# Computing the second branch gate in the recurrent block and parking it in DRAM

## The reference

```python
u = rms_norm_2(h, norm_mix_g[l])
proj = u @ w_in[l]
x_rnn, g_rnn, q_c, kv_c, k_pe, gate_logits = jnp.split(proj, split_points, axis=-1)
xa = causal_conv(x_rnn, conv_w[l], conv_b[l])
ya = rg_lru(xa, ...) * jax.nn.gelu(g_rnn)
yb = mla(q_c, kv_c, k_pe, positions, ...)
gates = jax.nn.sigmoid(gate_logits.astype(jnp.float32)).reshape(B, S, N_BRANCH, D_MODEL)
merged = gates[:, :, 0] * ya.astype(jnp.float32) + gates[:, :, 1] * yb.astype(jnp.float32)
h = h + merged.astype(h.dtype) @ w_out[l]
```

## Time and profile before

| | us |
|---|---|
| median of 3 runs | 3211.88 |
| lowest and highest | 3197.32, 3213.42 |
| profiled execution | 3216.03 |
| its span | 3214.2 |
| mean granted clock of TensorE | 0.942 |

### The profile page before, as it was taken

The page is one execution under the profiler, slowest core; times in us unless marked ns, Lnnn a source line. Parts: engine busy times, 40 slices in busy tenths (PEclk is TensorE's granted clock), DMA queues, the critical chain, the costliest instruction groups (busy, mean ns, idle before and its releaser), DMA issues. The chain is left out here.

```text
span 3214.2 us, 35213 instructions
## 1 busy us (share of the span) xinstructions
PE 2864.6 (89%) x13216; PEld 2177.6 (68%) x13216; DVE 1801.3 (56%) x2575; ACT 1037.1 (32%) x1329; POOL 211.3 (7%) x186
## 2 busy tenths in 40 slices
PE   4999999999999997949998979899999989479993
PEld 3887778787877884737776955657565568357772
DVE  4677777877632313264444257667575773456663
ACT  3233332333321213244444122212131231246661
POOL 0010111100100000000000010000000000422213
PEclk8999999999999997969999979999999999689996
DMA  4332212232325110121110200000100111779996
GB/s 142 115 108 96 95 66 96 97 109 77 126 97 187 47 33 23 30 92 37 43 46 27 70 14 22 14 22 1 36 1 14 53 35 68 284 250 350 353 362 244
DMA packets 167102, 319.82 MB, mean 100 GB/s; under 512 B 17511, under 2 KB 125160, under 8 KB 153240
## 3 DMA queue, kind: packets, MB, share of 16 engines
q1 hardware_dynamic: 151352, 279.81, 25.3%
q0 software_dynamic: 14720, 34.64, 2.8%
q10 hardware_dynamic: 864, 3.15, 0.2%
HBM read 288.70 MB, written 95.96 MB: 120 GB/s over the span
## 5 line engine op out<-in xcount | busy, mean ns | idle before, releaser
L464 PE MATMUL PS<-UHI,WHI 128*128 128x512 f32 x1008 | 415.4, 412 | 30.0 <-DVE arena L786 15.5
L464 PE MATMUL PS<-ULO,WHI 128*128 128x512 f32 x1008 | 402.6, 399 | 0.0
L464 PE MATMUL PS<-UHI,WLO 128*128 128x512 f32 x1008 | 402.4, 399 | 0.0
L464 PEld LDWEIGHTS PS<-UHI,WHI 128*128 128x128 f32 x1008 | 191.8, 190 | 82.0 <-issue 39.2
L464 PEld LDWEIGHTS PS<-ULO,WHI 128*128 128x128 f32 x1008 | 192.0, 191 | 46.9 <-issue 4.1
L464 PEld LDWEIGHTS PS<-UHI,WLO 128*128 128x128 f32 x1008 | 191.7, 190 | 46.8
L127 DVE TENSOR_TENSOR WLO<-arena,WHI 128x1024 fp32r<-128x1024 f32 x88 | 107.4, 1222 | 190.2 <-ACT WHI L123 190.0
L1940 ACT ACTIVATE arena<-PS,small 128x128 f32<-128x128 f32 (+7 forms) x128 | 94.8, 741 | 241.5 <-DVE small L2013 241.5
L1371 PE MATMUL PS<-U2HI,WHI 128*128 128x512 f32 x384 | 156.2, 407 | 14.0 <-DVE WLO L127 13.9
L1838 PE MATMUL PS<-arena 96*128 96x512 f32 (+3 forms) x384 | 163.4, 539 | 3.7 <-DVE arena L2000 2.9
L800 DVE SCALAR_TENSOR_TENSOR RC<-arena,cols,RC 128x1024 f32<-128x1024 f32 x120 | 157.4, 1312 | 9.9 <-issue 0.5
(11 more groups left out here) (437 smaller groups left out, 5693.5 us busy)
## 6 DMA issues: line engine op xcount, KB each, us to landing
arena<-in_w_in SPq DMA_DIRECT2D x88, 512.0 KB, 3.9
xd_dram<-in_x SPq DMA_DIRECT2D x32, 768.0 KB, 6.4
y_dram<-in_x SPq DMA_DIRECT2D x32, 768.0 KB, 6.1
arena<-in_w_gate SPq DMA_DIRECT2D x13, 1024.0 KB, 7.2
arena<-in_w_up SPq DMA_DIRECT2D x13, 1024.0 KB, 10.2
arena<-in_w_down SPq DMA_DIRECT2D x13, 1024.0 KB, 13.1
arena<-in_w_out SPq DMA_DIRECT2D x32, 256.0 KB, 2.8
RB<-in_w_gate SPq DMA_DIRECT2D x7, 1024.0 KB
```

The costliest lines, as they stand in the source:

```text
L464: last = pe.matmul(o[:, h * HALF:(h + 1) * HALF], x[:, k, :], y[:, k, h * HALF:(h + 1) * HALF], start=(k == r == 0), stop=(k == ND - 1 and ...
```

## The change

The recurrent block now projects eight tiles for each b (NX = 8): the two new ones are the second gate's tiles, from the split input like the others. ScalarE's sigmoid of them goes to SIGB, and SyncE stores it to a DRAM tensor. The attention block loads the finished gate from there. The plain matmuls, their sigmoids, and the re-addition of the two halves of the input (whole) go away. The counts of all semaphores go from 6 to 8 for each block.

```diff
-        XCOLS = [0, P, D, D + P, GATE0_COL, GATE0_COL + P]
+        XCOLS = [0, P, D, D + P, GATE0_COL, GATE0_COL + P, GATE1_COL, GATE1_COL + P]
+        SIGB = [SQUARES[:], part(23 * T + 8, (T,))]
+        sig1_dram = nc.dram_tensor("sig1_dram", [ND, P, T], F32).ap()
...
+                def store_gate(b, t):
+                    sp.wait_ge(s_revac, NX * b + 7 + t)
+                    hold(sp)
+                    sp.dma_start(sig1_dram[ds(2 * b + t, 1)].rearrange("a p t -> (a p) t"), SIGB[t]
+                                 ).then_inc(s_sigst[t], 16)
...
                 with sp.Fori(1, NB) as b:
-                    for n in range(6):
-                        sp.wait_ge(s_rwlo, 6 * b + n - 1)
+                    for n in range(NX):
+                        sp.wait_ge(s_rwlo, NX * b + n - 1)
                         hold(sp)
                         load(b, n)
-                    sp.wait_ge(s_ri, 2 * b)
-                    hold(sp)
-                    load_gates(b)
+                        if 1 <= n <= 2:
+                            store_gate(b - 1, n - 1)
+                        if n == 2:
+                            sp.wait_ge(s_ri, 2 * b)
+                            hold(sp)
+                            load_gates(b)
+                for t in range(2):
+                    store_gate(NB - 1, t)
+                for t in range(2):
+                    sp.wait_ge(s_sigst[t], 16 * NB)
...
-                    project(b, 4)
-                    project(b, 5)
+                    for n in range(4, NX):
+                        project(b, n)
...
+                    elif n >= 6:
+                        if later:
+                            act.wait_ge(s_sigst[t], 16 * b)
+                        act.activation(SIGB[t], pair, ACT.Sigmoid).then_inc(s_revac, 1)
...
                         dve.tensor_tensor(INP[t], INP[t], REC[t], ALU.mult)
-                        if more:
-                            lower(b + 1, t)
+                        if t == 0:
+                            lower(b, 6)
+                        elif more:
+                            lower(b + 1, 0)
...
                         dve.tensor_tensor(RA[:, ds(2 * b + t, 1), :].rearrange("p a t -> p (a t)"), REC[t],
                                           SIG[t], ALU.mult).then_inc(s_mt, 1)
+                        if t == 0:
+                            lower(b, 7)
+                        elif more:
+                            lower(b + 1, 1)
...
-                pool.wait_ge(s_lproj, 3 * NT)
-                for k in range(5, ND):
-                    last = whole(pool, k)
-                last.then_inc(s_whole, 1)
...
-                for k in range(5):
-                    last = whole(dve, k)
-                last.then_inc(s_whole, 1)
...
                 def load_gate(g):
                     for t in range(2):
-                        w = a["w_in_2"].rearrange("o (k p) n -> p (o k) n", p=P)
-                        sp.dma_start(WGATE[t], w[:, :, ds(g * 256 + GATE1_COL + t * P, P)]).then_inc(s_w1, 16)
+                        sp.dma_start(SIG1[t], sig1_dram[ds(2 * g + t, 1)].rearrange("a p t -> (a p) t")
+                                     ).then_inc(s_sigland, 16)
...
-                    pe.wait_ge(s_w1, 32 * g + 32)
-                    for t in range(2):
-                        for h in range(2):
-                            for k in range(ND):
-                                last = pe.matmul(banks(4 + 2 * t)[:, h * HALF:(h + 1) * HALF], WGATE[t][:, k, :],
-                                                 RC[:, k, h * HALF:(h + 1) * HALF],
-                                                 start=(k == 0), stop=(k == ND - 1))
-                        last.then_inc(s_g1, 1)
                     pe.wait_ge(s_rot, g + 1)
...
-                    pe.wait_ge(s_g1sig, 2 * g + 2)
                     scores(g, 0)
...
-                    for t in range(2):
-                        act.wait_ge(s_g1, 2 * g + t + 1)
-                        act.activation(SIG1[t], banks(4 + 2 * t), ACT.Sigmoid).then_inc(s_g1sig, 1)
...
+                    dve.wait_ge(s_sigland, 32 * g + 32)
+                    hold(dve)
                     dve.wait_ge(s_yturn, g + 1)
```

More of the change, by code:

```diff
@@ L1306, in build @@
         GATE0_COL = 2 * D + 768 + 256 + 32
+        GATE1_COL = GATE0_COL + D
+        NX = 8
         RPAD = [part(k * (T + 4), (T + 4,))[:, 0:T + 3] for k in range(2)]
@@ L1316, in build @@
         one = small[:, 65:66]
-        XCOLS = [0, P, D, D + P, GATE0_COL, GATE0_COL + P]
+        XCOLS = [0, P, D, D + P, GATE0_COL, GATE0_COL + P, GATE1_COL, GATE1_COL + P]
+        SIGB = [SQUARES[:], part(23 * T + 8, (T,))]
+        sig1_dram = nc.dram_tensor("sig1_dram", [ND, P, T], F32).ap()
+        s_sigst = [sem(f"s_sigst{k}") for k in range(2)]
         s_rland = [sem(f"s_rland{k}") for k in range(2)]
@@ L1363, in project @@
                 def project(b, n):
-                    pe.wait_ge(s_rwlo, 6 * b + n + 1)
+                    pe.wait_ge(s_rwlo, NX * b + n + 1)
                     if n >= 2 or not isinstance(b, int):
-                        pe.wait_ge(s_revac, 6 * b + n - 1)
+                        pe.wait_ge(s_revac, NX * b + n - 1)
                     o = banks(2 * (n % 2))
@@ L1404, in upper @@
                 def upper(b, n):
-                    act.wait_ge(s_rland[n % 2], 48 * b + 16 * (n // 2) + 16)
+                    act.wait_ge(s_rland[n % 2], 8 * NX * b + 16 * (n // 2) + 16)
                     split_hi(act, WHI5[n % 2][:], WRAW5[n % 2]).then_inc(s_rwhi, 1)
@@ L1409, in evacuate @@
                     evacuate_one(b, n)
-                    if more or n < 4:
-                        upper(b + (n + 2) // 6, (n + 2) % 6)
+                    if more or n < NX - 2:
+                        upper(b + (n + 2) // NX, (n + 2) % NX)
                 def evacuate_one(b, n):
-                    act.wait_ge(s_rproj, 6 * b + n + 1)
+                    act.wait_ge(s_rproj, NX * b + n + 1)
                     t, pair, later = n % 2, banks(2 * (n % 2)), not (isinstance(b, int) and b == 0)
@@ L1453, in block_of @@
                         act.activation(THMUL[t], THMUL[t], ACT.Sqrt, scale=2.0).then_inc(s_mroot, 1)
-                    evacuate(b, 4, more)
-                    evacuate(b, 5, more)
+                    for n in range(4, NX):
+                        evacuate(b, n, more)
                 act.wait_ge(s_soft, 1)
@@ L1501, in lower @@
                 def lower(b, n):
-                    dve.wait_ge(s_rwhi, 6 * b + n + 1)
+                    dve.wait_ge(s_rwhi, NX * b + n + 1)
                     hold(dve)
@@ L1509, in body @@
                         lower(b, 2 + t)
-                        dve.wait_ge(s_revac, 6 * b + t + 1)
+                        dve.wait_ge(s_revac, NX * b + t + 1)
                         hold(dve)
@@ L1537, in body @@
                         dve.drain()
-                        dve.wait_ge(s_revac, 6 * b + 5 + t)
+                        dve.wait_ge(s_revac, NX * b + 5 + t)
                         dve.tensor_tensor(REC[t], REC[t], GELU[t], ALU.mult)
@@ L1578, in build @@
         s_w6used = sem("s_w6used")
-        s_whole = sem("s_whole")
         s_lproj = sem("s_lproj")
@@ L1589, in build @@
         s_trig = sem("s_trig")
-        def whole(eng, k):
-            return eng.tensor_tensor(RC[:, k, :], U2HI[:, k, :].bitcast(F32), U2LO[:, k, :].bitcast(F32), ALU.add)
         with nc.Block() as block:
@@ L1617, in _ @@
                     load(n)
-            @block.gpsimd
-            def _(pool):
-                pool.wait_ge(s_lproj, 3 * NT)
-                for k in range(5, ND):
-                    last = whole(pool, k)
-                last.then_inc(s_whole, 1)
             @block.tensor
@@ L1739, in evacuate @@
                 def evacuate(m):
-                    if m == 0:
-                        dve.wait_ge(s_whole, 2)
                     dve.wait_ge(s_lturn, m + 1)
@@ L1763, in build @@
         NG, GH, NTASK = 4, 4, 4 * NT
-        GATE1_COL = GATE0_COL + D
         SCALE = 96 ** -0.5
@@ L1774, in build @@
         VTOK = part(19 * T + 512, (NT, GH, 64))
-        WGATE = [part(21 * T + 512 + k * T, (ND, P)) for k in range(2)]
         SIG1 = [part(21 * T + 512 + k * T, (T,)) for k in range(2)]
@@ L1780, in build @@
         rowrec = small[:, 212:214]
-        s_w1 = sem("s_w1")
+        s_sigland = sem("s_sigland")
         s_w8 = sem("s_w8")
@@ L1787, in build @@
         s_kev = sem("s_kev")
-        s_g1 = sem("s_g1")
-        s_g1sig = sem("s_g1sig")
         s_qms = sem("s_qms")
```

## The result

The changed kernel took 3277.74 us (median of 4 runs, 3275.12 to 3279.74), the kernel before 3212.65 in the same runs: a ratio of 1.0213, 95% interval 1.0181 to 1.0245. It is slower by 65 us. I had forecast slower by 92 and a time of 3304 in a range of 3282 to 3328: the side is right, the size is off by 27 us, and the time lies 4 us under the range. The profiled execution of the changed kernel took 3276.92 us (span 3274.8), 60.6 us of span more than before.

The account below looks back on a forecast made before the run. TensorE was taken to bound the recurrent block, VectorE's chain to cover attention's gate matmuls. Terms 88.8 + 0.2 - 4.6 - 6.5 + 12 + 2.7 = +92.6 us gave 3304 us, range 3282 to 3328 (8 in 10).

Parts of the forecast that it names:

- Eight more projections: Recurrent block: eight added projections at 11.1 us each on TensorE's path, +88.8 us, plus 0.2 for a last-block stall.
- rival E: Recurrent block: VectorE's new order makes low parts late and stalls TensorE, about 8 us a passage, +24, 3329 us; chance 0.06.
- The block's end: End of each recurrent block: only the last sigmoid and its store remain before the next load, 5.0 for 9.6 us, -4.6.
- whole removed: End of the latent block: without VectorE's five additions the square root and all behind it come earlier, -6.5 us.
- The gate's matmuls hidden: Attention: the gate's matmuls lie beneath VectorE's rotary chain, so removing them saves 0 us on the path.
- The transposes at low clock: Attention: after TensorE's idle time the 64 transposes start at half speed, 3 us a group, +12 us in four groups.
- Rival B: Attention: all 64 transposes stay at half speed and group one's scores begin low, +115.4 us, 3327 us; chance 0.16.
- The scores: Attention scores: half of one further 5.5 us low-clock stretch, since group one might get one or others lose theirs, +2.7 us.
- rival C: Attention scores: the low stretch disappears because a clock just risen does not fall, +73.4 us, 3285 us; chance 0.13.

Follow-up runs that it names:

- early re-additions: Kernel before with six of eight re-additions of the split input moved into VectorE's idle time, two left to GpSimd: 3201.0 us, ratio 0.9973.
- filling: Changed kernel with 32 unused matmuls put back into TensorE's 28 us of idle time in each attention group: 3279.48 us, ratio 1.0226 to the kernel before.
- thinning: Kernel before with only one, or six, of eight k steps of the gate's matmuls in attention: 3202.19 us (ratio 0.998), or 3200.45 us (0.9978).

## Why the prediction was right in its sign and wrong in its size

*Eight more projections, +88.8 and +0.2.* Right. The first projection to the last matmul took 328.82 us and now takes 418.17: +89.3. One pass instead of three gave 43 us back. VectorE's new waits stalled nothing: rival E did not occur.

*The block's end, -4.6.* Right; from the last projection's last matmul to the first of the latent block 13.80 became 8.11, -5.7.

*whole removed, -6.5.* Right; from the last latent matmul to the transposes 14.95 became 8.56, -6.4; shown alone by the early re-additions.

*The gate's matmuls hidden.* Right, shown from both sides: filling and thinning leave the transposes' release with VectorE.

*The transposes at low clock, 4 x 3.* Right kind, too large: 9.41 - 7.73 = 1.7 us in the first group, 1.8 in the last, 7 in all. The clock rose 3.7 to 4.2 us after the first transpose, and from then on they ran at 1.00. I had taken the middle between two rows, and the larger of them came from transposes with gaps between. Rival B is out: all four groups reached 1.00 within them. So this trace does not agree with the sentence in the Trainium skill, "TensorE: Matmul & The Clock Gate", Part 4, that full speed does not engage for transposes.

*The scores, "I take half of one: +2.7".* This is the step that failed. The low stretch left all three groups that had it and came to none: in each of them the distance went from 102.9 to 99.1 us, which is -5.5 for the stretch and +1.7 for the transposes. In sum the stretches gave -16.5 us, so this term was off by 19. That alone would have given 3285, inside my range; the transposes' 5 us on top put the time under it. It is rival C, at 0.13, whose 3285 is nearest to what came. I saw that group one had no stretch, and that gaps came ahead of the fall; I held them for its cause whatever came before. The profiles show a fall only where two things meet: TensorE at full clock since before the transposes, and both gaps open. There the clock fell in 14 of 16 groups, for 3.4 to 23.8 us (the two profiles of before, the filled idle time, the early re-additions). With a matmul in either gap, or with 7.4 us or more of idle ahead of the transposes, it fell in none of 36. Group one of the kernel before has both and no fall, so they are not the whole cause.

*What I did not forecast:* -6.8 us after attention. It is no part of the change: in the other kernels, all with the same code from there on, this stretch took 568 to 573 us, the unchanged kernel again 572.5, and 576.0 in the profile of before was the longest of all. A sum made against one profile took that as fixed; the 4.1 us that I subtracted to get from the profile to the runs made up for part of it. The stretch holds waits for transfers, one of 16.20 us before and 12.96 after.

## What to carry to other kernels

Matmuls that end before another engine's chain does cost nothing on the path, so moving them to a stage where TensorE is the bound costs them in full, whatever it does to TensorE's busy time. When a change makes TensorE idle, price the clock twice: the slow start, and what the clock then does not do later; a group of the same loop that lacks a low stretch says that this stretch can go. Look for low clock in windows before any restructuring: here one matmul without use in a gap of 0.9 us lowered the median by 14 us, more than the change saved in attention (10) or in the latent block (6.4). Where the runs of one kernel fall into two groups, look at their mean clocks and profile one of each before building on one profile.

## What the runs showed of the hardware

- The granted clock fell from 1.00 to 0.50 for 13.6 us, with TensorE busy for 13.50 of 13.60 us. It had just done 64 transposes at 1.00 and stood in the second of two gaps of 0.9 us. Over the 14 groups with such a fall in four profiles it set in 10.4 to 11.6 us after the first transpose, and lasted 13.6 us in seven, 3.4 us in six and 23.8 us in one.
- With one unused matmul (two records, 0.85 us of time) in either gap or in both there was no fall in 16 groups of 16 (four kernels), where the kernel before had one in three groups of four.
- After 7.4 to 28 us of idle the transposes began at 0.50, the clock rose to 1.00 within them, and no fall followed in the scores in any of 20 groups of five kernels (distances of 98.96 to 99.54 us); 16 of these groups had both gaps open. Why a clock that has just risen stays up through the same gaps is open.
- Two profiles of the same kernel had their long stretches in the same three groups, to 0.03 us. Yet its 67 other runs came in two kinds, 3197 to 3205 us at a mean clock of 0.945 to 0.948 and 3208 to 3220 us at 0.942 to 0.944. What picks the kind, and which groups fall in another kernel, is open.
